# A hybrid encoder layer on one core: fewer scratch bytes, an earlier start of attention, and other places for tile 0's rows

## What is computed

```
xn = rmsnorm(x);  z = xn @ w_in      # q | k | v | f | i | qb | g | gate_a | gate_b
o_a = band attention(q, k, v) with bias rel_bias[h, clip(dist, -256, 256) + 256], softmax over keys
o_b = gated linear recurrence (chunks of 64), per-head rmsnorm, silu(g)
h  = x + (sigmoid(gate_a) * (o_a @ w_a) + sigmoid(gate_b) * (o_b @ w_b)) @ w_out
q  = rmsnorm(h) @ w_query;  s = q . sub_keys;  16 best of 128 x 128 key pairs, for 8 heads
y  = h + sum over 8 heads x 16 experts of gate * gelu(rmsnorm(h) . u[idx]) * v[idx]
y  = rmsnorm(y) * norm_final
```

## Time and profile before

| | before |
|---|---|
| median of 3 runs | 3772.97 us (3766.97 to 3773.9) |
| the profiled execution | 3773.11 us, its span 3771.3 us |
| busy share: PE, DVE, ACT, POOL | 82%, 71%, 23%, 59% |
| bytes moved | 1409.65 MB, mean 374 GB/s |
| chain that ended last | PE 37%, DMA 26%, DVE 17%, POOL 9% |

### The profile page before, as it was taken

How to read it: one execution, slowest core, us unless ns; L and a number is a source line. 1 busy time by engine, 2 the same in 40 slices (tenths; PEclk the granted TensorE clock), 3 DMA queues, 4 the chain that set the end, 5 groups by cost and what they waited for, 6 DMA issues and landing times.

```text
span 3771.3 us, 35324 instructions
## 1 busy us (share of the span) xinstructions
PE 3099.5 (82%) x11076; PEld 1822.5 (48%) x11076; DVE 2685.9 (71%) x5855; ACT 873.4 (23%) x2073; POOL 2224.4 (59%) x2224
## 2 busy tenths in 40 slices
PE   5869988897788998987889998976888998876555
PEld 4756746553456555542567465533565455321112
DVE  0345677689876696699786776798685765887775
ACT  2222222122232231222331321222232212221101
POOL 0022544566766575666665674667675755777775
PEclk7987999999999999999989999998899999997888
DMA  6687879999999999999999999999999999999998
GB/s 184 212 307 241 321 282 329 379 406 392 389 389 403 395 405 403 408 407 379 396 389 402 391 407 405 407 388 378 395 397 402 410 401 387 395 410 409 410 410 334
DMA packets 443263, 1409.65 MB, mean 374 GB/s; under 512 B 46528, under 2 KB 48064, under 8 KB 442312
## 3 DMA queue, kind: packets, MB, share of 16 engines
q0 software_dynamic: 316960, 1152.82, 78.6%
q1 hardware_dynamic: 101520, 201.08, 14.5%
q10 hardware_dynamic: 24600, 53.51, 4.1%
HBM read 1389.91 MB, written 19.95 MB: 374 GB/s over the span
## 4 chain that ended last, share of the span: by engine, by line
PE 37%; DMA 26%; DVE 17%; POOL 9%; issue 8%; ACT 2%; ACTq 0%; DVEq 0%; POOLq 0%
PE PS L670 16%; DMA ring<-in_peer_v,idx 15%; PE PS L988 11%; POOL ring L650 9%; DMA wring<-in_w_in 7%; DVE ring L1790 6%; PE PS L674 5%; DMA ring<-in_peer_u,idx 2%; PE PS L841 1%; PE PS L764 1%; PE PS L789 1%; DMA wring<-in_w_out 1%; DVE acc L1801 1%; DVE arena L1457 1%; DMA wring<-in_peer_query 1%
## 5 line engine op out<-in xcount | busy, mean ns | idle before, releaser
L988 PE MATMUL PS<-ring,diag 128*128 128x512 f32 (+1 forms) x3032 | 1548.8, 645 | 423.5 <-DMA ring<-in_peer_v,idx 391.9
L1790 DVE CUSTOM_DVE_ANT_0 ring<-ring,PS 128x1024 f32<-128x1024 f32 x1088 | 1312.3, 1213 | 272.3 <-DMA ring<-in_peer_u,idx 263.4
L650 POOL DMA_INDIRECT ring<-in_peer_u,idx x1088 | 1096.7, 1008 | 681.5 <-PE PS L988 311.5
L650 POOL DMA_INDIRECT ring<-in_peer_v,idx x1088 | 1107.2, 1018 | 626.5 <-DVE hid L1790 336.7
L988 PEld LDWEIGHTS PS<-ring,diag 128*128 128x128 f32 (+1 forms) x3032 | 557.7, 198 | 1208.4 <-issue 988.7
L670 PE MATMUL PS<-xnT,wring 128*128 128x256 f32 (+2 forms) x3840 | 763.1, 358 | 56.1 <-DMA wring<-in_w_in 37.7
L670 PEld LDWEIGHTS PS<-xnT,wring 128*128 128x128 f32 x3840 | 672.2, 198 | 175.1 <-issue 49.9
L1801 DVE SCALAR_TENSOR_TENSOR acc<-ring,wk,acc 128x1024 f32<-128x1024 f32 x330 | 424.6, 1287 | 67.1 <-issue 38.8
L1362 ACT ACTIVATE diag<-masks,wk 128x128 f32<-128x128 f32 x704 | 260.4, 396 | 662.6 <-PE PS L988 504.7
L674 PE MATMUL PS<-wring,xnT 128*128 128x512 f32 (+1 forms) x432 | 195.0, 604 | 10.1 <-DMA wring<-in_w_in 10.0
L1553 DVE SCALAR_TENSOR_TENSOR arena<-PS,arena 128x256 f32<-128x256 f32 (+4 forms) x72 | 47.8, 664 | 138.0 <-PE PS L764 85.1
(11 more groups left out here) (223 smaller groups left out, 2469.3 us busy)
## 6 DMA issues: line engine op xcount, KB each, us to landing
wring<-in_w_in SPq DMA_DIRECT2D x110, 1024.0 KB, 12.1
wring<-in_peer_query SPq DMA_DIRECT2D x40, 1024.0 KB, 11.7
wring<-in_w_out SPq DMA_DIRECT2D x20, 1024.0 KB, 11.9
ring<-in_peer_u,idx POOLq DMA_INDIRECT x1088, 12.9
ring<-in_peer_v,idx POOLq DMA_INDIRECT x1088, 13.1
arena<-rel_scr ACTq DMA_DIRECT2D x80, 144.0 KB, 6.3
wring<-in_w_branch_a SPq DMA_DIRECT2D x10, 1024.0 KB, 16.7
wring<-in_w_branch_b SPq DMA_DIRECT2D x10, 1024.0 KB, 13.8
```

Source lines behind the costliest of these rows:

```text
L650: pool.indirect_dma_start(ring[:, SLOT[n], :], None, u_tab if kind == "u" else v_tab, bass.IndirectOffsetOnAxis(ap=idx[:, at:at + 1], axis ...
L988: mm = pe.matmul(PS[0:rows, 6 + half, :], diag[:, seq % ND, 0:rows], ring[:, SLOT[n], 512 * half:512 * (half + 1)], start=(seq == pe_of[tn ...
L1790: dve.tensor_tensor_reduce(row, row, xp_row, 1.0, 0.0, ALU.mult, ALU.add, hid[:, m % 2, k:k + 1]).then_inc(dve_used, 1)
```

## The change

Six edits go together.

1. `rel_scr` keeps 384 columns per row instead of 640. Each head's bias has the value of its far end subtracted; what lies further away is then zero and is set once per group by two more memsets. A head's loads become 2 x 80 KB. The raw table is loaded contiguously as ScalarE's first transfer, and VectorE reverses it.
2. In group 0 the first bias loads are issued ahead of v's copy; `lb` is computed after attention; the sub-keys are turned head by head in F, in PSUM banks 6 and 7.
3. For the weights of group 0 up to H there are six slots: the three of `wring` and three pairs of ring slots, which hold no rows yet. The sub-keys follow behind the sixth block and lie in ring slots too.
4. The first tile of groups 0 to 3 (tiles 0, 1, 3, 5) no longer goes through DRAM: H writes h straight into `acc` and xn into `xt`, and the row steps wait for that. In groups 0 and 1 x is loaded into `acc` once and not again in H. `xt` has one buffer instead of two.
5. The final gain is loaded once, in group 1's A, into `gain_f`.
6. `slices(1)` multiplies the costs of group 1's stages.

```diff
+    more = dict(B=1.5, C=0.8, D=1.9, E=1.9, F=0.55, G=1.8, H=1.2) if g == 1 else {}
+    before = [(s, x * more.get(s, 1.0)) for s, costs in zip("ABCDEFGHI", (a, b, c, d, e, f, gg, h, [4.0])) for x in costs]
...
+def kept(g, ti):
+    return ti == 0 and GROUPS[g][ti][0] != SAMPLE
+def weight_slots(n, early):
+    last, uses = [-1] * NWE, [0] * NWE
+    slot, turn, before = [], [], []
+    for b in range(n):
+        s = min(range(NWE if b < early else NW), key=lambda x: (last[x], x))
...
+def x_of(g, s, ti):
+    if kept(g, ti) and g < 2 or s == "H+" and kept(g, ti):
+        return acc[:, tiles_to(g) % 2, :]
+    return hx[:, ti, :]
...
     # SyncE
-                if b >= NW:
-                    sp.wait_ge(pj_ready, last_product[b - NW] + 1)
+                if block_before[b] is not None:
+                    sp.wait_ge(pj_ready, last_product[block_before[b]] + 1)
-                if b == NW - 1:
+                if b == NWE - 1:
                     sp.dma_start(sk, ...)
     # GpSimd
-            pool.dma_start(rel_scr, bass.AP(rel_line.tensor, 127, [[768, HA], [-1, P], [1, WIN]]))
+            pool.dma_start(rel_scr, bass.AP(rel_line.tensor, 127 + WIN - NEAR, [[768, HA], [-1, P], [1, NEAR]]))
+                if via_acc[tn]:
+                    return
+                pool.wait_ge(h_out, h_landed[g + 1])
+                if tn >= 1:
+                    pool.wait_ge(xp_made, 2 * tn)
     # TensorE, in F of group 0, after each head's state product
+                            for k in range(4):
+                                mm = pe.transpose(PS[:, 6 + h % 2, k * P:(k + 1) * P], sk[:, 4 * h + k, :], ident[:, :])
     # ScalarE
-                for t0, j0 in ((0, 0), (64, 64)):
-                    act.dma_start(bias[t0:t0 + 64, bh % 2, j0:j0 + 576], rel_scr[h, t0:t0 + 64, j0:j0 + 576])
+                for t0 in (0, 64):
+                    j0 = WIN - NEAR + t0
+                    act.dma_start(bias[t0:t0 + 64, bh % 2, j0:j0 + 320], rel_scr[h, t0:t0 + 64, t0:t0 + 320])
-                    act.wait_ge(const_in, 32)
+                    act.wait_ge(ss_set, 1)
                 act.wait_ge(x_in, x_tiles[g, "A"])
+                    if g == 0 and what == "v":
+                        act.wait_ge(rel_out, 16)
+                        load_bias(g, 0)
+                        load_bias(g, 1)
-                    act.dma_start(h_scr[tid * P:tid * P + rows, :], hx[0:rows, ti, :])
+                    if not kept(g, ti):
+                        act.dma_start(h_scr[tid * P:tid * P + rows, :], hx[0:rows, ti, :])
-                        act.dma_start(xt[:, s, :], bass.AP(norm_final.tensor, 0, [[0, P], [1, D]]))
     # VectorE, in H
+                if kept(g, 0) and T >= 2:
+                    dve.wait_ge(y_out, 16 * (T - 1))
...
+                if kept(g, 0) and T >= 1:
+                    dve.wait_ge(xp_made, 2 * T)
+                if kept(g, 0) and T >= 2:
+                    dve.wait_ge(e_sq, T - 1)
```

More of the change, by code:

```diff
@@ L72, in last_head, with through @@
     return q + 1 == HEADS or HEAD[q + 1][1] == 0
+def kept(g, ti):
+    return ti == 0 and GROUPS[g][ti][0] != SAMPLE
+def through(g):
+    return sum(1 for q in range(g) for ti in range(len(GROUPS[q])) if not kept(q, ti))
 def tiles_to(g):
@@ L95, in slices @@
     h = [1.7] * (4 * nt) + [0.5, 2.5, 0.5, 1.5, 3.0] + [1.5] * nt
-    before = [(s, x) for s, costs in zip("ABCDEFGHI", (a, b, c, d, e, f, gg, h, [4.0])) for x in costs]
+    more = dict(B=1.5, C=0.8, D=1.9, E=1.9, F=0.55, G=1.8, H=1.2) if g == 1 else {}
+    before = [(s, x * more.get(s, 1.0)) for s, costs in zip("ABCDEFGHI", (a, b, c, d, e, f, gg, h, [4.0])) for x in costs]
     if g == 0:
@@ L304, in plan_projections @@
     return blocks, sets, products, parts
+def weight_slots(n, early):
[3 more added lines that the diff above has]
+        s = min(range(NWE if b < early else NW), key=lambda x: (last[x], x))
+        slot.append(s)
+        turn.append(uses[s])
+        before.append(last[s] if uses[s] else None)
+        uses[s] += 1
+        last[s] = b
+    return slot, turn, before
 def build(nc, x_prompt, x_sample, cache_k, cache_v, state_in, norm_mix, w_in, rel_bias, lb_logits,
@@ L312, in build @@
     blocks, sets, products, parts = plan_projections()
+    early = sum(len(mine) for mine, _, _, first, _ in sets if products[first][0] == 0 and products[first][1] != "I")
+    block_slot, block_turn, block_before = weight_slots(len(blocks), early)
     last_product = {}
@@ L481, in build @@
         rel = arena[0:HA, 12 * WG:12 * WG + 767]
-        sk = cut(arena[:, 0:2048], 16, P)
-        skTs = part(3072, 16, P)
+        rel_raw = arena[0:HA, 16 * WG:16 * WG + NREL]
+        sk = cut(ring[:, 0:2, :].rearrange("p a b -> p (a b)"), 16, P)
+        skTs = cut(ring[:, 2:4, :].rearrange("p a b -> p (a b)"), 16, P)
+        lb_in, ss_set = sem("lb_in"), sem("ss_set")
         const_in, rel_in, sk_in, relE, rel_out, sk_tr, sk_cp, sk_out, consts, lb_d, lb_a, state_loaded = [
@@ L490, in build @@
         merged = sem("merged")
-        w_in_sem = [sem(f"w_landed{n}") for n in range(NW)]
+        w_in_sem = [sem(f"w_landed{n}") for n in range(NWE)]
         pj_ready = sem("pj_ready")
@@ L558, in build @@
         s_slot = (tile_ids[stn + 1] + 1) % 2
-        xt_landed = [sum(48 if tile_ids[t] == SAMPLE else 32 for t in range(tn % 2, tn + 1, 2)) for tn in range(NT)]
+        via_acc = [kept(g, ti) for g in range(NG) for ti in range(len(GROUPS[g]))]
+        xt_landed = [sum(48 if tile_ids[t] == SAMPLE else 0 if via_acc[t] else 32 for t in range(tn % 2, tn + 1, 2))
+                     for tn in range(NT)]
         def list_at(q):
@@ L565, in build, with xn_of @@
         tile_at = [(g, ti) for g in range(NG) for ti in range(len(GROUPS[g]))]
+        xn_done = [norm_no[g, "H", ti] + 1 for g, ti in tile_at]
         k_tiles = {g: [ti for ti, (tid, _, _) in enumerate(GROUPS[g]) if tid >= 4] for g in range(NG)}
         kt_before = {g: sum(len(k_tiles[q]) for q in range(g)) for g in range(NG + 1)}
-        x_tiles = {(g, s): 16 * (2 * tiles_to(g) + (2 if s == "H" else 1) * len(GROUPS[g]))
-                   for g in range(NG) for s in "AH"}
+        x_tiles, loads = {}, 0
+        for g in range(NG):
+            loads += len(GROUPS[g])
+            x_tiles[g, "A"] = 16 * loads
+            loads += len(GROUPS[g]) - (1 if g < 2 else 0)
+            x_tiles[g, "H"] = 16 * loads
+        h_landed = [32 * through(g) for g in range(NG + 1)]
+        def x_of(g, s, ti):
+            if kept(g, ti) and g < 2 or s == "H+" and kept(g, ti):
+                return acc[:, tiles_to(g) % 2, :]
+            return hx[:, ti, :]
+        def xn_of(g, s, ti):
+            return xt[:, :] if s == "H" and kept(g, ti) else xn[:, ti, :]
         @block.sync
@@ L1810, in unit @@
                     dve.wait_ge(dve_used, latest[0])
-                    dve.wait_ge(xt_in[s], xt_landed[m])
+                    if not via_acc[m]:
+                        dve.wait_ge(xt_in[s], xt_landed[m])
                     for half in range(2):
```

157 lines of the change are left out of this document (87 added, 70 removed).

## The result

The changed kernel takes 3718.14 us (median of 4 runs, 3711.16 to 3720.37) against 3772.05 for the kernel before: a ratio of 0.9856, 95% interval 0.9839 to 0.9873, or about 54 us less. The forecast was 3700, with 3668 to 3740 for 8 in 10. The profiled execution has a span of 3714.9 us, 56.4 less than before, and moved 1389.72 MB.

The account below looks back on a forecast made before the run. Bytes bound the third part; before it, a chain of waits or one engine. Start -28, tile 0's rows -12, bytes -31 and end -1.8 sum to -73 from 3773.1, giving 3700 us, with 3668 to 3740 for 8 in 10.

Parts of the forecast that it names:

- Bytes, forecast -31: After 700 us: 14.2 MB fewer bias, gain and scratch transfers, 35.7 us at 397 GB/s, taken as -31 us.
- cut by 53/61: Bytes term scaled down because 8 of 61 windows after 700 us were counted at a DMA share of 1.00 or less.
- the bytes were hidden: Rival, third part: norms, stores and gain loads ran in slack, a third of the term remains, -10, 3721 us; chance 0.12.
- Start, forecast -28: Start: earlier norm -8.0, no weight-block stop -8.6, earlier bias loads -8.0, two weight waits -3.4; together -28 us.
- Six weight blocks go out at once, so the stop of 8.57 goes: First projection in the start: its stop for the fourth weight block disappears, -8.6 us.
- The two weight waits of -3.4: Later in the start: waits on weight blocks of 1.74 and 1.68 us go with the deeper prefetch.
- Tile 0's rows, forecast -12: Beside group 1's mix: F -17, D and E +3, G and H +3, C -1; sum -12 us.
- In F, VectorE is the bound, so 15 times 1.29 is 19.4, of which I take -17: Group 1's F: 15 fewer u rows, each priced at its VectorE and read-out time, save 17 us.
- the row shift pays nothing: Rival: VectorE waits for rows ahead of gate products, TensorE for banks; tile 0 costs +20, time 3732 us; chance 0.12.
- The clock, a rival: TensorE in D, E, G, H: half of 173 us at the lower clock, 87 us more, time 3787; chance 0.05.
- The bias table was not late: Rival, start: table's write stays late beside six weight blocks, start gives only -12, time 3716 us; chance 0.12.
- More than forecast: Rival: even spread regains half the missing DMA share, tile 0 gives -32, start -34, time 3674 us; chance 0.05.

Follow-up runs that it names:

- The experiment with the bytes back: Changed kernel with the final gain loaded per tile, tiles 3 and 5 through scratch and the bias 576 wide again: 3754.0 us, ratio 0.9937.
- the emptied F: Changed kernel with F's multiplier lowered from 0.55 to 0.03, tile 0's rows there falling from 16 to 2: 3729.93 us in one run.
- the run without the shift: Changed kernel without edit 6, the multipliers of group 1's stage costs left empty: 3714.44 us, ratio 0.9838.
- the narrow run: Changed kernel with the norm's gain asked for ahead of the raw bias row and group 0 loading only the bias columns it reads: 3714.25 us, one run.

## Why the prediction came out in its range, and which steps were wrong

*Bytes, forecast -31 and -1.8 with the end: right.* The stretch from group 1's second norm to the end lost 34.8 us. The experiment with the bytes back gives the price alone, 1.8 to 2.4 us per MB. The measured value lies between the term as cut by 53/61 (-32.8 with the end) and uncut (-37.5), and single profiles of this part differ by 6 us, so they do not tell whether the cut was right. The count behind it was misread: the row shown for 3200 us has a DMA share of 1.03 (its 1.00 is the clock), and 7 windows, not 8, stand at 1.00 or less; that makes -31.6 of the -31. The rival "the bytes were hidden" is refuted.

*Start, forecast -28: -24.8, near in sum, with one wrong reason and some luck.* The norm came 7.8 us earlier as forecast, but the first projection only 6.9, because the gain of the norm is now late: it took 10.8 us to land instead of 4.5, as it now stands second on ScalarE's queue, and nothing covers it. The stop of 8.57 us went, and 12.3 with the slower matmuls around it, which the sum did not have; these 3.7 us made up for more than half of what failed to come elsewhere. But the step "Six weight blocks go out at once, so the stop of 8.57 goes" named the wrong sole cause. Three slots with an early table do without the stop as well; late and wide, the table brings it back, two blocks further on. The stop was a meeting of the fourth block's load with the table's write. The bias loads gave 8.4 for 8.0. What the sum lacked is the later heads' bias loads: I looked at the first two, which were moved, and not at what the other six would meet (+2.7 in attention). The two weight waits of -3.4 did not show in the sum of the later stages (+0.1). Against them stands at least a wait for `in_peer_query` in group 0's I, 5.1 us after and 3.1 before; the rest of this balance was not tested. What the earlier norm, the place of the first bias loads and the resident gain gave is read from the two traces; no run undid them one by one.

*Tile 0's rows, forecast -12: +3.1, the term that failed.* It failed at "In F, VectorE is the bound, so 15 times 1.29 is 19.4, of which I take -17". VectorE was busy for 107.84 of 115 us there, and I took a full engine for the bound. It was full because the order had filled the chain's gaps with rows. Taken out, most of them left gaps: 24.3 us less work, 8.7 us less time, and a floor of 102 us that the emptied F shows. Of the other half of the term, D and E at +3 measured +3.9 and G and H at +3 measured +6.5, twice as much, half of it as slower matmuls. So the rows were moved from where they cost 0.6 us each to where, by the run without the shift, a pair costs some 0.5 (6.8 us for 13 pairs in D and E) to 1 us (5.9 for 6 in G and H). The working had part of the reason at hand: it put D and E's transfers at 97 us of TensorE's 101. The rival "the row shift pays nothing" named the side, and its +20 was too dear. Of its path the traces show little: VectorE waited only 1.9 us for rows in D and E, and TensorE waited there for weight blocks, not for banks; in G and H 2.4 us of it show.

*The clock, a rival: refuted in its size.* D and E were granted 1.00. G and H, from F's end to the second norm, were granted 0.90 instead of 0.96, which is 3.4 us of TensorE's time and not 87. Its argument against itself misread a row: VectorE was not nearly idle in D and E before, but busy for 55.17 of 106 us.

*The other rivals.* The bias table was not late: the first biased score came at 38.82 us. "More than forecast" did not come either: the DMA share of F fell from 0.82 to 0.60 and that of C from 0.74 to 0.62.

The total lies in the range because the bytes, the largest term, came as forecast. It is 18 us above the forecast: 15 from the rows and 3 from the start, 2 back from the bytes, and 1 to 2 between the profiled execution (3716.88) and the median.

## What to carry to other kernels

An engine that is 94% busy beside a chain of dependent steps may be full of filler: before taking work away from it, ask what the stage would last without the filler, and price a moved piece by the slope of the stage's time, not by the piece's length on its engine. Here filler cost nothing in B, where TensorE is the bound and the transfers have room (a DMA share of 0.69), up to 28 us of VectorE's work; with 33.56 us B grew to 47.80. It cost some 0.5 us a pair in D and E and 1 us in G and H, where the DMA share was already 0.89 and 0.98. Bytes, on the other hand, count for most or all of their time where the DMA share stands at 1. When the first load of a series is moved ahead, look at what the later ones of the series will meet.

## What the runs showed of the hardware that was not expected

Emptying F slowed what remained on TensorE. The granted clock of F fell from 0.90 to 0.81 and, emptied, to 0.60, a mixture of the levels of 1.2 and 2.4 GHz. The same 96 matmuls of F (columns: count, busy, mean ns, idle before) took 15.1 us, 318 ns each, in the kernel before; here they are in the changed kernel and with F emptied:

```profile
L894 PE MATMUL PS<-arena 128*128 128x128 f32 x96 | 15.4, 321 | 4.8 <-DVE arena L1697 4.7
```

```profile
L894 PE MATMUL PS<-arena 128*128 128x128 f32 x96 | 22.8, 427 | 3.7 <-DVE arena L1697 3.7
```

At 0.81 they were hardly slower; at 0.60, where nearly all of the v rows that stand between them on TensorE were gone, they took 7.4 us longer. They stand in the chain of every head, so some 7 us of F's floor of 102 us are this (an estimate from these two rows); what F would last at the full clock was not tried.

A small load can be slow without being large, by its place on its queue. The gain, 4 KB, took 4.5 us to land in the kernel before and 4.6 in the narrow run, where it is ScalarE's first transfer, and 10.8 in the changed kernel, where it is the second, behind 16 KB. The weight blocks beside it do not explain this: with three of them asked for instead of six it took 10.8 us as well. The logits, 4 KB too, took 10.9 us as the second transfer and 19.3 as the third.
